# Three slots for split weights and splits made two pieces ahead, in a two-block transformer kernel

## What is computed

```
for l in range(2):                        # first block
    proj = rms_norm(x, norm_g[l]) @ w_in[l]
    ...                                   # three kinds of attention, a low-rank projection
    x = x + mixed @ w_out[l]
c_act = silu(c)                           # second block
mod = c_act @ w_ada + b_ada               # six rows, and two more from w_ada_final
h = modulate(rms_norm(x, g_mix), sh1, sc1)
proj = h @ w_in
...
x = x + gt1 * (o @ w_out)
y = hier_moe(modulate(rms_norm(x, g_ffn), sh2, sc2), w_gate, w_up, w_down)
```

## Time and profile before

| | us |
|---|---|
| median of 3 runs | 2558.75 (2557.39 to 2564.81) |
| the profiled execution | 2550.7, of it the span 2548.9 |
| first block, both layers | about 0 to 1110 |
| second attention | about 1110 to 1525 |
| routing and gathering | about 1525 to 1590 |
| 32 experts | about 1590 to 2528 |
| PE busy | 2269.9 (89% of the span) |
| DVE busy | 1414.1 (55%) |
| ACT busy | 726.7 (29%) |

### The profile page before, as it was taken

The page is one execution under the profiler, slowest core; times in us unless marked ns, Lnnn a source line. Parts: engine busy times, 40 slices in busy tenths (PEclk is TensorE's granted clock), DMA queues, the critical chain, the costliest instruction groups (busy, mean ns, idle before and its releaser), DMA issues. The chain is left out here.

```text
span 2548.9 us, 37257 instructions
## 1 busy us (share of the span) xinstructions
PE 2269.9 (89%) x14757; PEld 1673.6 (66%) x14757; DVE 1414.1 (55%) x2015; ACT 726.7 (29%) x1347; POOL 44.2 (2%) x66
## 2 busy tenths in 40 slices
PE   6999999889999998969989896999888888888886
PEld 5789988768799987758778675544444444444442
DVE  3778798765778898854544555333333333333334
ACT  2444444333443445344544433000000000000001
POOL 0100000000100000011000000000000000000000
PEclk8999999997999999989999997999999999999998
DMA  5877766764877666864434325999999999999997
GB/s 195 307 286 290 282 245 256 268 239 189 337 285 291 263 258 238 327 230 146 141 125 149 116 98 203 401 422 422 422 422 422 422 422 422 422 422 422 422 422 318
DMA packets 109410, 762.55 MB, mean 299 GB/s; under 512 B 12369, under 2 KB 16241, under 8 KB 17521
## 3 DMA queue, kind: packets, MB, share of 16 engines
q1 hardware_dynamic: 109152, 760.21, 75.3%
q10 hardware_dynamic: 144, 0.79, 0.1%
HBM read 758.00 MB, written 2.95 MB: 299 GB/s over the span
## 5 line engine op out<-in xcount | busy, mean ns | idle before, releaser
L2260 PE MATMUL b_ps<-s_raw,s_window 128*64 128x256 f32 x4096 | 460.9, 382 | 58.8 <-DVE x_tokens L2486 39.2
L2260 PEld LDWEIGHTS b_ps<-s_raw,s_window 128*64 128x64 f32 x4096 | 295.4, 137 | 235.9 <-issue 72.6
L1141 DVE TENSOR_TENSOR s_w_tail<-s_raw,s_w_head 128x1024 fp32r<-128x1024 f32 x292 | 345.0, 1223 | 86.1 <-ACT s_w_head L742 85.8
L927 PE MATMUL b_ps<-s_h_head,s_w_head 128*128 128x256 f32 x1184 | 343.3, 290 | 13.8 <-DVE s_w_tail L1141 13.8
L742 ACT ACTIVATE s_w_head<-s_raw 128x1024 fp32r<-128x1024 f32 x292 | 292.5, 1050 | 188.3 <-DMA s_raw<-in_w 176.4
L928 PE MATMUL b_ps<-s_h_tail,s_w_head 128*128 128x256 f32 x1184 | 336.2, 284 | 0.0
L929 PE MATMUL b_ps<-s_h_head,s_w_tail 128*128 128x256 f32 x1184 | 336.1, 284 | 0.0
L1218 DVE SCALAR_TENSOR_TENSOR s_ada_acc<-s_raw,s_c_col,s_ada_acc 128x2048 f32<-128x2048 f32 x120 | 282.3, 2353 | 0.0
L2280 PE MATMUL b_ps<-s_raw,s_diag 128*64 128x512 f32 x1024 | 238.0, 600 | 39.5 <-DMA s_raw<-in_w_down 24.3
L927 PEld LDWEIGHTS b_ps<-s_h_head,s_w_head 128*128 128x128 f32 x1184 | 228.0, 193 | 29.2 <-DVE s_w_tail L1141 17.5
L928 PEld LDWEIGHTS b_ps<-s_h_tail,s_w_head 128*128 128x128 f32 x1184 | 228.3, 193 | 0.1
(11 more groups left out here) (340 smaller groups left out, 3174.2 us busy)
## 6 DMA issues: line engine op xcount, KB each, us to landing
s_raw<-in_w SPq DMA_DIRECT2D x198, 1024.0 KB, 5.0
s_raw<-in_w_ada SPq DMA_DIRECT2D x128, 1024.0 KB, 7.2
s_raw<-in_w_gate SPq DMA_DIRECT2D x128, 1024.0 KB, 24.1
s_raw<-in_w_up SPq DMA_DIRECT2D x128, 1024.0 KB, 26.5
s_raw<-in_w_down SPq DMA_DIRECT2D x128, 1024.0 KB, 26.6
x_tokens<-in_x SPq DMA_DIRECT2D x1, 2048.0 KB, 7.7
s_rel<-in_rel SPq DMA_DIRECT2D x1, 2048.0 KB, 12.2
s_raw<-mod_rows SPq DMA_DIRECT2D x2, 1024.0 KB, 12.3
```

The source lines that it names most:

```text
L927: pe.matmul(out, head, m_head, start=first, stop=False, skip_group_check=True)
L1141: dve.tensor_tensor(w_tail[:, i % SPLITS, cols], raw[:, slot["w", i], cols], w_head[:, i % SPLITS, cols].bitcast(F32), ALU.subtract)\
L2260: ins = pe.matmul(psum[64 * h:64 * h + 64, c // 4, 0:T], window[:, 4 * (c % 4) + k, :], raw[:, c, k * 512 + h * T:k * 512 + h * T + T], st ...
```

## The change

Two constants change, and one argument: `w_head` and `w_tail` get three slots each, in step i ACT and DVE split piece i + 2 instead of piece i + 1 (step 0 splits pieces 1 and 2), and the room for the third slots comes from a scratch area of the compiler for transfers whose descriptors are made by software. The kernel issues all its transfers from SP and ACT. RAW stays 5, and the stream and its waits stay as they are.

```
-SPLITS = 2
-AHEAD = 1
+SPLITS = 3
+AHEAD = 2
...
-    nc = bacc.Bacc("TRN2", target_bir_lowering=False, num_devices=1)
+    nc = bacc.Bacc("TRN2", target_bir_lowering=False, num_devices=1, dynamic_dma_scratch_size=1024)
```

## The result

| | before | after |
|---|---|---|
| median, us | 2560.32 (4 runs, 2557.39 to 2564.81) | 2966.69 (4 runs, 2963.64 to 2970.79) |
| the profiled execution, us | 2550.7, span 2548.9 | 2970.8, span 2969.0 |
| mean PE clock | 0.967 | 0.905 |

The change makes the kernel slower by 406 us, ratio 1.160 (95% interval 1.1575 to 1.1622). The forecast was 2959 us, in a range of 2890 to 3060.

A forecast was written before the change was run, and what follows sets the result against it. The prediction took a one-step loop through a transfer to bound the first block after the change: 2550.7 + 403.4 for both layers' stretches - 3.4 = 2950.7 us, 2959 us as median with 8 us carried over; range 2890 to 3060.

The forecast's parts named there:

- the loop: First block: ada add frees a slot, load, head split, tail, next ada; spanning two steps before, one after.
- The count of positions: Stream order with five raw slots: the load of w(i+2) waits for ada(i-1), where w(i+1) waited for ada(i-2).
- The turn: One pass ada start to ada start: 2.38 to issue, 4.76 to head split, 1.09 to tail, 2.27 to ada; 10.50 us.
- The paying steps: First-block steps that each hold a full turn: 55 a layer, in four stretches, 574.2 us after correcting three short ones.
- DVE work ahead of the ada piece: DVE work between tail and ada piece lengthens the turn: 23.5 us a layer, 10 either way.
- the two large terms: The low-rank norm in step 11 and the rotation in step 38, each put at 4.9 us of DVE work.
- DVE work behind the ada piece: Costs nothing: the longest regular case, 3.9 us, lies under the 5.85 us of the next landing and head split.
- The 40.2 us for tails: PE's first-block waits for split tails, 34 places before; forecast no gain, becoming longer waits of about 4 us a step.
- the price of 0 to 40 us: Lower PE clock after pauses costs at most 2 us in each of 10 heads a layer coupled to PE's scores.
- PE at its low clock as the bound: Third rival: PE work in paying steps at 1.2 GHz exceeds the turn; 3060 us up, up to 3256; chance 8%.
- The 3.4 us of the second attention: One PE wait for a tail there, where no ada pieces share the stream; forecast as saved by the change.
- The first rival: The change does what it says: PE's 43.6 us of tail waits go, giving about 2515 us; chance 4%.

The follow-up runs named there:

- e5: The kernel before with each ada piece one place earlier in the stream, ahead of its weight piece; two slots, splits one piece ahead: 2985.4 us, ratio 1.1686.
- e2: The changed kernel with its stream of loads put in the order in which pieces are read: 2511.3 us, ratio to before 0.9826.
- e4: The changed kernel, stream as it was, with DVE adding its ada piece ahead of the tails instead of behind them: 2534.0 us, ratio to before 0.9936.
- e6: The changed kernel with DVE adding only 1024 of 2048 columns from a sum's second ada piece on, loads whole: 2848.6 us, ratio to before 1.1155.
- e9: The changed kernel with each gate's reciprocal, DVE work behind the ada piece, taken over 16 of 256 columns: 2959.2 us, ratio to before 1.1583.
- e8: The kernel before with three slots and splits two pieces ahead in the second attention alone: 2550.2 us, ratio to before 0.9995.
- e1: The kernel before with the third split slots and smaller scratch alone, splits still one piece ahead: 2553.6 us, ratio to before 0.9994.
- e7: The kernel before with six slots of raw instead of five in the first block, two setup semaphores merged: 2532.9 us, ratio to before 0.9922.

## Why the prediction was right, and where it was off

**What bounds the kernel, and the loop.** Right, and shown from four sides: the same loop made in the kernel before (e5), taken out of the changed one by the stream (e2) and by DVE's order (e4), and shortened by one link (e6). The count of positions was the step on which all depended.

**The turn.** Forecast 10.50 us, measured 10.65 in the rows above and 10.57 to 10.80 in the first six turns. The whole difference is the transfer, the term taken at 4.76 from one event and found at 4.91; the other links are within 0.01. At 0.15 us too little, 110 turns are 16.5 of the 25.2 us by which the two sums after were underestimated (611.41 and 609.17 against 597.7 each).

**The paying steps.** Of the 55 intervals between ada starts in the four stretches of layer 1, none is shorter than 9.5 us, and right behind the four stretches they are 4.5 to 8.1 us. So 55 turns a layer is right.

**DVE work ahead of the ada piece.** Forecast 23.5 us a layer, with 10 either way. The turn of step 11 was 15.1 us and that of step 38 15.7, so the two large terms at 4.9 each measured 4.4 and 5.1. The sum of a layer less 55 turns of 10.65 and with 3.3 back for the short ones leaves 29 us in layer 1 and 27 in layer 2. In the fourth stretch (turns of 11.4 to 13.8 at C heads and adds to x) it is about 10 where 8 was put. In layer 1 another 3 us are no work of DVE at all: two turns of 12.28 and 12.03 in the second stretch, whose load took 6.20 and 6.29 us to the head split instead of 4.91. DVE work behind the ada piece costs nothing, as said (e9).

**The waits of PE.** The 40.2 us for tails did become a longer wait, but not the "about 4 us a step" that stood in the list of signs: 127.7 us in 37 places for tails, and 120.8 in 18 places at the scores (L1073), which the profile puts down to no releaser and which were 5.7 us before; together 2.3 us a turn. In the stretches of layer 1 PE stood idle for 3.0 us a turn in all (611.41 less 445.61, over 55). Part of its slack went into a lower clock: it is busy for 445.61 us instead of 374.24, 1.3 us more a turn where 2.4 was estimated.

**The clock.** No run changed the clock alone, so the price of 0 to 40 us is neither shown nor refuted. A turn of 10.65 adds up from DVE, SP, the transfer and ACT, with no PE link in it, so by these rows the clock costs nothing in the regular steps. Whatever it costs in the heads that need PE's scores is inside the 29 and 27 us above. The rival, PE at its low clock as the bound, is refuted by e6: with PE's work unchanged the time fell one for one with the ada piece.

**What was taken at nothing.** Outside the stretches 13.1 us were gained where nothing was forecast for the first block; that the split two ahead brings a little where the stream has slack fits this, but no run tried it. The 3.4 us of the second attention are borne out by the traces together (under e8), and not by this pair. Slots and scratch are free within 3 us (e1).

**A base read wrong.** The prediction took 395.56 us of the earlier trace rows for the same four stretches of layer 2. With 391.03 its growth would have been 4.5 us more, and the forecast 2963 to 2964.

**The sum.** For the profiled execution the forecast was 2950.7 us, and it took 2970.8: 20.1 us more. The growth of the stretches was 29.8 us too low (433.2 against 403.4; about 16.5 of it the transfer, 8.7 the extra time in the turns, 4.5 the wrong base), 13.1 were gained outside them, and the 3.4 of the second attention did not show: 29.8 - 13.1 + 3.4 = 20.1. Against the median only 7.7 us are left (2966.7 - 2959), because 8.3 were added to the sum to pass from the profiled execution to the median, and the profiled execution of after lay 4.1 over its own median: 20.1 - 8.3 - 4.1 = 7.7. So the nearness of 7.7 us owes something to luck: the mechanism and the size of the turn were right, and the errors that were left cancelled in part.

**The first rival** (it does what it says, 2515 us) named the right prize for another kernel: e2, which changes the stream as well, measured 2511.3.

## To carry to other kernels

When two kinds of pieces share one ring of slots, load them in the order in which they are read, and redo that order whenever a reading distance changes. For each load ask which piece frees its slot and how many steps earlier that piece is read: if it is one step, and that piece is read only behind a split that itself waits for a load, every step holds a full transfer. Looking further ahead in one kind of piece can bring the use of its loads that close; here it cost 16.0%, where the same constants with a re-ordered stream gave 1.7%. When the order of the stream cannot change, the order of reading can (e4), or the ring can get one slot more (e7, measured on the kernel before).

## What the runs showed of the hardware

- *A load's time.* A weight piece of 1 MB with an ada piece issued 0.38 us behind it and nothing older in flight took 4.91 us from issue to the head split. The medians to landing on the page of the profile in the changed kernel are 4.9 us for a weight piece (the 52 of the second attention, which have no ada piece, are among them) and 7.0 for an ada piece. From these medians I estimate that the second of a pair lands 2.5 us behind the first (7.0 + 0.38 - 4.9), which is 1 MB at about 420 GB/s, the rate of the experts. So by these numbers the two land one after the other, and the first isn't slowed to half by the second. Landing times of the changed kernel, page, transfers with count, size and median us:

```profile
s_raw<-in_w SPq DMA_DIRECT2D x198, 1024.0 KB, 4.9
s_raw<-in_w_ada SPq DMA_DIRECT2D x128, 1024.0 KB, 7.0
```

  The Trainium skill, "DMA: Bandwidth & Descriptors", section "Anatomy of one DMA — SWDGE (gpsimd) path", gives 2.0 us plus the bytes at 436 GB/s for transfers on the GpSimd path, which would make 4.4 us for 1 MB, an estimate. The loads here are issued from SP, and the trace has 4.9, somewhat more.

- *The clock after a pause.* PE in the changed kernel, in order of time, matmuls of one piece behind a wait of 4.20 us:

```profile
855.48 0.50 PE L927 MATMUL b_ps<-s_w_head,s_h_head 128*128 128x512 f32 x1 [4.20 <-DVE s_w_tail L1141]
...
857.40 0.63 PE L927 MATMUL b_ps<-s_w_head,s_h_head 128*128 128x512 f32 x1
857.83 0.63 PE L928 MATMUL b_ps<-s_w_tail,s_h_head 128*128 128x512 f32 x1
...
859.93 0.39 PE L927 MATMUL b_ps<-s_w_head,s_h_head 128*128 128x512 f32 x1
860.16 0.39 PE L928 MATMUL b_ps<-s_w_tail,s_h_head 128*128 128x512 f32 x1
```

  From 857.40 matmuls start 0.43 us apart, the pace of 1.2 GHz, and from 859.93 every 0.23 us, that of 2.4 GHz, within one piece. The first ones after the wait, from 855.48, aren't slow yet, which the earlier trace rows didn't show. It differs from pause to pause: behind one of 3.42 us the matmuls from 106.19 on were slow at once, until 112.33, and behind one of 2.01 us, at 116.84, none was. The Trainium skill, "TensorE: Matmul & The Clock Gate", section "Why this matters for your kernels", warns of such pauses; the trace agrees that the clock falls (mean 0.905 against 0.967), but in the regular turns it was paid for out of PE's own slack, which still left 3.0 us of idle time a turn.
